# The experts' stage of a mixer-and-experts block: ten precomputed activation blocks spread over 64 groups, and loaded into another tensor

## The chip, the cores and the metric

The kernel runs on one core of a Trainium2 chip. The metric is device time in microseconds, the median of three runs. Besides, one execution was profiled, and the rows below are from it. Engines are named as in the profile: PE (TensorE), DVE (VectorE), ACT (ScalarE), POOL (GpSimd) and SP (SyncE, whose queue issues most plain loads and stores).

## The reference, cut to what matters

One layer: a token mixer, a LayerNorm, and a feed-forward part that retrieves single-neuron experts. Only the last concerns us. With `x` the 1024 tokens of width 1024 behind the first LayerNorm, each token picks 128 of 16384 experts (8 heads, 16 each) with gates, and

```python
def expert_block(args):
    xb, eb, gb = args
    h = jnp.einsum('td,ted->te', xb.astype(f32), u[eb].astype(f32))
    a = jax.nn.gelu(h, approximate=False) * gb
    return jnp.einsum('te,ted->td', a, v[eb].astype(f32))
```

The output is LayerNorm(alpha * x + that), with float32 throughout.

## The kernel before

**Two ways for two halves of the tokens.** The kernel treats 512 tokens sparsely and 512 densely. The four tiles of 128 sparse tokens gather their U and V rows from HBM, one row for each token and picked expert: `gather_u` and `gather_v` on POOL's queue, 128 rows of 4 KB (512 KB) in one indirect DMA. VectorE forms the dot products with the U rows (`dot_rows`, L2147), TensorE sums the V rows of three tiles (`weigh_rows`, L2001, one step for each four gathers), and VectorE those of the last tile (`sum_rows`, L2156). U rows have a ring of 4 buffers and V rows one of 8.

The 512 dense tokens go through all 16384 experts, with gates that are zero where an expert wasn't picked. The experts are cut into 128 blocks of 128, two to a group, so there are 64 groups. In a group `g`, for `j` = 0 and 1:
- SP loads the U block (512 KB) into `e_ur`, ScalarE and VectorE split it into a high part `e_uh` (L2029) and a low part `e_ul` (L2101), one group ahead. TensorE forms the hidden product in 24 matmuls (`hidden`, L1953 to L1955: high x high, high x low, low x high), and ScalarE its Gelu into `e_a` (L2046).
- VectorE multiplies by the gates (`weigh`, L2117), which SP loads as one 512 KB block into `e_g`. ScalarE and VectorE split the product in `e_a` (L2041, L2122).
- SP loads the V block (512 KB) into the single `e_vr`, which is split likewise (L2035, L2105).
- TensorE multiplies the two and VectorE adds eight PSUM banks into `e_y` (`values`, L1986 to L1988, 48 matmuls a group, run one group later; `gather`, L2137).

**What is computed ahead.** 20 of the 128 blocks (`AHEAD`) have had their hidden product and Gelu before this stage, in the retrieval (12) and the gates' stage (8), where they are stored to the scratch tensor `hidden` in HBM. In the kernel before these are blocks 0 to 19, and so groups 0 to 9 (`SHORT` = 10) are short: their `weigh` takes the activations from `e_ur`, where SP loads two blocks of 256 KB (`load_u`, L1859), and TensorE, ScalarE and VectorE skip the product, the Gelu and the splits of U. From group 10 on `load_u` fetches the U blocks (L1864).

**The order of work.** The groups run in the order of their numbers, and each engine has its instructions for a group written out by hand. The rows of the sparse tiles are spread over four phases of the groups, `PHASE = (0, 18, 36, 53, 64)`: in the first three phases each group gets some seven U gathers with their dot products and some seven V gathers, and at a phase's end the sums are turned into the next tile. In the last phase VectorE sums the V rows of the fourth tile, some 12 a group. The SP queue, in order, for each group: the U loads of the next group, the gates, V for `j` = 0, (in the short groups: the next activations), V for `j` = 1. Each waits for the engine that frees the buffer, and holds up what is behind it.

Of the kernel before, what the change touches and what calls it, by code (L numbers as in the profile page):

```python
# [36 lines left out]
TG = 64  # L37
# [17 lines left out]
AHEAD = AHEAD_R + AHEAD_G  # L55
LEVELS = 7

# [1050 lines left out]
def retrieve(nc, sem, io, scr, cst, psum, x1s, x1d, hold, w0, key1, key2, gate):  # L1108
# [3 lines left out]
    with ExitStack() as ctx:  # L1112
# [473 lines left out]
def build_gates(nc, sem, io, scr, cst, psum, x1d, hold, pickT, id_u, hs):  # L1586


    with ExitStack() as ctx:
# [32 lines left out]
        with nc.Block() as block:  # L1622
# [139 lines left out]
def experts(nc, sem, io, scr, cst, psum, x1d, hold, id_u, id_v, gate_s, hs, out):  # L1762
# [3 lines left out]
    with ExitStack() as ctx:  # L1766
# [4 lines left out]
        SHORT = AHEAD // 2  # L1771
# [25 lines left out]
        ln_in = 16 * (NG + 1)  # L1797

        u_in = [sem(f"u_in{j}") for j in range(2)]
        v_in = [sem(f"v_in{j}") for j in range(2)]  # L1800
# [52 lines left out]
        with nc.Block() as block:  # L1853
            @block.sync
            def _(sp):
                def load_u(g, j):
                    if g < SHORT:
                        sp.wait_ge(a_mul[j], g)
                        sp.dma_start(ur[j].rearrange("p k e -> p (k e)")[:, 0:TD],  # L1859
                                     scr["hidden"][2 * g + j]).then_inc(u_in[j], 16)  # L1860
                    else:
                        sp.wait_ge(a_mul[j], SHORT)
                        sp.wait_ge(u_lo[j], g - SHORT)
                        sp.dma_start(ur[j][:], io["uT"][2 * g + j]).then_inc(u_in[j], 16)  # L1864
# [10 lines left out]
                for j in range(2):  # L1875
                    load_u(0, j)
                for g in range(NG):
                    if SHORT < g + 1 < NG:
# [4 lines left out]
                    if g + 1 <= SHORT:  # L1883
                        for j in range(2):
                            load_u(g + 1, j)
                    load_v(g, 1)
                    if g == 0:
                        for t in range(ND):
                            sp.dma_start(y[:, t, :], scr["x1"][TS + t * P:TS + (t + 1) * P, :]).then_inc(x1_in, 16)
                for j, src in enumerate(("ln2_g", "ln2_b")):  # L1890
                    sp.wait_ge(u_lo[j], NG - SHORT)
# [55 lines left out]
            def _(pe):  # L1947
                def hidden(g, j):
                    pe.wait_ge(u_hi[j], g - SHORT + 1)
                    pe.wait_ge(u_lo[j], g - SHORT + 1)  # L1950
                    pe.wait_ge(gelu[j], g - SHORT)
# [61 lines left out]
                for g in range(NG + 1):  # L2013
                    for c in range(V_SLOTS):
                        if c < 2 and SHORT <= g < NG:
                            hidden(g, c)
# [8 lines left out]
            def _(act):  # L2025
                def split_u(g, j):
                    act.wait_ge(u_in[j], 16 * (g + 1))
                    act.wait_ge(h_mm[j], g - SHORT)
# [14 lines left out]
                def activate(g, j):  # L2043
                    act.wait_ge(h_mm[j], g - SHORT + 1)
# [21 lines left out]
                for g in range(NG):  # L2066
# [7 lines left out]
                    for j in range(2):  # L2074
                        if g >= SHORT:
                            activate(g, j)
                        split_a(g, j)
                        if SHORT <= g + 1 < NG:
# [274 lines left out]
```

## Time and profile before

| | us |
|---|---|
| median of 3 runs | 3144.13 |
| lowest and highest | 3140.07, 3150.45 |
| the profiled execution | 3145.47 |
| its span in the profile | 3143.8 |

The span runs from the first to the last instruction that the profile shows. A "busy" time counts instructions of the engine itself, without waits. PE's matmuls overlap, so that a matmul's duration is longer than the distance from its start to the next one's; where the rows below give a length of work on PE or DVE, starts are compared.

### The profile page before, as it was taken

Reading aid. Unit: us, or ns where it says so; the run is one execution under the profiler, and the core shown is the slowest. Engines: PE = TensorE matmul, PEld = TensorE weight load, DVE = VectorE, ACT = ScalarE, POOL = GpSimd, SP = SyncE. Lnnn points to the kernel's source line nnn. Section 1 sums busy time; section 2 is a strip of 40 time slices with the busy share of each in tenths; the row PEclk is TensorE's granted clock in tenths of the full one; section 3 lists DMA queues with packets and bytes.
Section 4 is the critical chain, followed back from the end, with each engine's and each line's share of the span. In section 5 each row is a group of like instructions: output and inputs, shape, how many; then the busy total and the mean of one; then the engine's idle time right before and its main releaser. Section 6 shows DMA issues by size and latency. Waiting matters only on the chain.

```text
span 3143.8 us, 40677 instructions
## 1 busy us (share of the span) xinstructions
PE 2644.5 (84%) x14888; PEld 2060.2 (66%) x14888; DVE 2306.0 (73%) x4891; ACT 1052.3 (33%) x1647; POOL 1616.3 (51%) x1190
## 2 busy tenths in 40 slices
PE   7996688889997466653767999999999999999996
PEld 6886577777775456551445767676767766667775
DVE  4511566655999799984777777777777777879999
ACT  4311333433544477760112222322222222222322
POOL 0001001112887455545666765676665777765774
PEclk9988799999998788886888999999999999999998
DMA  4222412222111599989999999999999999998995
GB/s 137 94 88 79 128 43 85 85 82 74 63 51 33 167 317 310 302 279 365 395 385 386 386 383 347 381 387 388 392 384 341 408 399 407 400 406 297 374 374 202
DMA packets 309791, 833.42 MB, mean 265 GB/s; under 512 B 26112, under 2 KB 114624, under 8 KB 309600
## 3 DMA queue, kind: packets, MB, share of 16 engines
q0 software_dynamic: 150864, 548.60, 45.4%
q1 hardware_dynamic: 158736, 282.31, 25.7%
q8 instruction: 115, 1.88, 0.2%
q14 instruction: 76, 0.62, 0.1%
HBM read 771.93 MB, written 58.88 MB: 264 GB/s over the span
## 4 chain that ended last, share of the span: by engine, by line
DVE 14%; DMA 13%; POOL 12%; PE 9%; issue 7%; ACT 0%; POOLq 0%; DVEq 0%; ACTq 0%
DMA e_u_row<-in_u,ids 13%; POOL hold L1913 8%; POOL e_u_row L1904 4%; DVE e_u_row L2147 4%; DVE e_y L2137 2%; PE psum L1986 2%; DVE e_u_row L2156 1%; PE psum L1987 1%; PE psum L1988 1%; DVE e_vl L2105 1%; DVE e_ul L2101 1%; DVE hold L2156 1%; PE psum L1953 1%; PE psum L1955 1%; PE psum L1954 1%
## 5 line engine op out<-in xcount | busy, mean ns | idle before, releaser
L2147 DVE CUSTOM_DVE_ANT_0 e_u_row<-e_u_row,hold 128x1024 f32<-128x1024 f32 x384 | 467.6, 1222 | 267.9 <-DMA e_u_row<-in_u,ids 267.1
L1904 POOL DMA_INDIRECT e_u_row<-in_u,ids x384 | 489.0, 1273 | 339.9 <-DVE ids L2147 231.6
L1986 PE MATMUL psum<-e_vh,e_ah 128*128 128x512 f32 x1024 | 425.1, 415 | 128.0 <-DVE e_y L2137 95.9
L1913 POOL DMA_INDIRECT hold<-in_v,ids x384 | 442.9, 1153 | 143.9 <-issue 112.8
L1987 PE MATMUL psum<-e_vl,e_ah 128*128 128x512 f32 x1024 | 412.7, 403 | 0.0
L1988 PE MATMUL psum<-e_vh,e_al 128*128 128x512 f32 x1024 | 410.7, 401 | 0.0
L1986 PEld LDWEIGHTS psum<-e_vh,e_ah 128*128 128x128 f32 x1024 | 199.9, 195 | 238.5 <-DVE e_y L2137 131.9
L1953 PE MATMUL psum<-x1d,e_uh 128*128 128x512 f32 x864 | 341.3, 395 | 0.0
L1954 PE MATMUL psum<-x1d,e_uh 128*128 128x512 f32 x864 | 337.2, 390 | 0.0
L1955 PE MATMUL psum<-x1d,e_ul 128*128 128x512 f32 x864 | 336.3, 389 | 0.0
L2137 DVE TENSOR_TENSOR e_y<-e_y,psum 128x512 f32<-128x512 f32 x464 | 299.7, 678 | 20.6 <-PE psum L1988 20.5
L1633 PE MATMUL psum<-g_one,g_two 128*128 128x128 f32 x1024 | 171.0, 345 | 136.9 <-DVE g_one L1676 136.9
L1688 POOL DMA_INDIRECT hold<-in_u,ids x128 | 194.6, 1521 | 173.1 <-DVE ids L1662 125.9
L1633 PEld LDWEIGHTS psum<-g_one,g_two 128*128 128x128 f32 x1024 | 165.9, 258 | 149.8 <-issue 149.8
L2046 ACT ACTIVATE e_a<-psum 128x512 f32<-128x512 f32 x108 | 64.5, 597 | 567.0 <-PE psum L1955 566.9
L2035 ACT ACTIVATE e_vh<-e_vr 128x1024 fp32r<-128x1024 f32 x128 | 135.3, 1057 | 346.3 <-DMA e_vr<-in_v 338.6
L1988 PEld LDWEIGHTS psum<-e_vh,e_al 128*128 128x128 f32 x1024 | 199.8, 195 | 44.9
L1987 PEld LDWEIGHTS psum<-e_vl,e_ah 128*128 128x128 f32 x1024 | 200.3, 196 | 39.4
L1101 POOL TENSOR_TENSOR hold<-hold,m_lng 128x1024 f32<-128x1024 f32 x8 | 18.9, 2362 | 380.7 <-DVE hold L989 380.7
L2001 PE MATMUL psum<-hold,e_column 128*32 128x512 f32 x1536 | 187.8, 607 | 28.3 <-DMA hold<-in_v,ids 21.8
L1953 PEld LDWEIGHTS psum<-x1d,e_uh 128*128 128x128 f32 x864 | 162.3, 188 | 64.4 <-issue 31.0
L2041 ACT ACTIVATE e_ah<-e_a 128x512 fp32r<-128x512 f32 x128 | 80.9, 632 | 347.7 <-DVE e_a L2117 344.2
(399 smaller groups left out, 5648.8 us busy)
## 6 DMA issues: line engine op xcount, KB each, us to landing
e_vr<-in_v SPq DMA_DIRECT2D x128, 512.0 KB, 6.7
e_ur<-in_uT SPq DMA_DIRECT2D x108, 512.0 KB, 6.7
s_G<-g_tile SPq DMA_DIRECT2D x8, 4096.0 KB, 27.0
e_g<-s_G SPq DMA_DIRECT2D x64, 512.0 KB
ids<-in_w_ch SPq DMA_DIRECT2D x17, 512.0 KB, 3.9
s_ch<-p_out POOLq DMA_DIRECT2D x16, 512.0 KB, 4.0
hold<-in_wq SPq DMA_DIRECT2D x16, 512.0 KB, 4.3
hold<-in_v,ids POOLq DMA_INDIRECT x476, 8.5
```

The costliest lines, as they stand in the source:

```text
L1633: last = nc.tensor.matmul(psum[:, n // 4, (n % 4) * NK:(n % 4 + 1) * NK], one2[s][:, n, :], one1[s][:, n, :], start=True, stop=True)
L1688: pool.indirect_dma_start(out=ring[k % U_RING], out_offset=None, in_=io["u"], in_offset=bass.IndirectOffsetOnAxis(ap=id_u[:, 0, k:k + 1], ...
L1904: pool.indirect_dma_start(out=u_ring[n % U_RING][:], out_offset=None, in_=io["u"], in_offset=bass.IndirectOffsetOnAxis(ap=id_u[:, s, k:k + ...
L1913: pool.indirect_dma_start(out=v_ring[m % V_RING], out_offset=None, in_=io["v"], in_offset=bass.IndirectOffsetOnAxis(ap=id_v[:, t:t + 1], a ...
L1953: nc.tensor.matmul(psum[:, j, :], uh[j][:, k, :], x1d[0][:, k, :], start=(k == 0), stop=False)
L1954: nc.tensor.matmul(psum[:, j, :], uh[j][:, k, :], x1d[1][:, k, :], start=False, stop=False)
L1955: last = nc.tensor.matmul(psum[:, j, :], ul[j][:, k, :], x1d[0][:, k, :], start=False, stop=(k == KC - 1))
L1986: nc.tensor.matmul(acc, ah[s][j][:, r], vh[s][j][:, c], start=(first and j == 0), stop=False)
L1987: nc.tensor.matmul(acc, ah[s][j][:, r], vl[s][j][:, c], start=False, stop=False)
L1988: last = nc.tensor.matmul(acc, al[s][j][:, r], vh[s][j][:, c], start=False, stop=(final and j == 1))
L2137: add = nc.vector.tensor_tensor(y[:, t, c], y[:, t, c], psum[:, bank(g, q), :], ALU.add)
L2147: nc.vector.tensor_tensor_reduce(row, row, xs[:, s, :], 1.0, 0.0, ALU.mult, ALU.add, hs[:, s, k:k + 1]).then_inc(dotted, 1)
```

## The change

`READY` names the ten short groups, spread over the stage: 0, 9, 19, 28, 37, 45, 54, 57, 60 and 63. The blocks that the two earlier stages compute ahead are the blocks of these groups (`ready_block`). In the experts' stage `computed(g)` counts the full groups before `g` and takes the place of `g - SHORT` in the semaphores' values. The activations of a short group are loaded by `load_ready` into `e_a` (`av[j]`) itself, when VectorE has finished the last group's subtraction on it (`a_lo`), with semaphores of their own; the product with the gates is then made in place. The two loads stand in the SP queue before and after the second V load. U loads no longer wait for `a_mul`.

```diff
+READY = (0, 9, 19, 28, 37, 45, 54, 57, 60, 63)
+def ready_block(n):
+    return 2 * READY[n // 2] + n % 2
+def computed(g):
+    return g - len([r for r in READY if r < g])
...
-                    sp.dma_start(ur[:], io["uT"][b]).then_inc(u_in, 16)
+                    sp.dma_start(ur[:], io["uT"][ready_block(b)]).then_inc(u_in, 16)
...
-                    sp.dma_start(ur[:], io["uT"][AHEAD_R + b]).then_inc(u_in, 16)
+                    sp.dma_start(ur[:], io["uT"][ready_block(AHEAD_R + b)]).then_inc(u_in, 16)
...
                 def load_u(g, j):
-                    if g < SHORT:
-                        sp.wait_ge(a_mul[j], g)
-                        sp.dma_start(ur[j].rearrange("p k e -> p (k e)")[:, 0:TD],
-                                     scr["hidden"][2 * g + j]).then_inc(u_in[j], 16)
-                    else:
-                        sp.wait_ge(a_mul[j], SHORT)
-                        sp.wait_ge(u_lo[j], g - SHORT)
-                        sp.dma_start(ur[j][:], io["uT"][2 * g + j]).then_inc(u_in[j], 16)
+                    sp.wait_ge(u_lo[j], computed(g))
+                    sp.dma_start(ur[j][:], io["uT"][2 * g + j]).then_inc(u_in[j], 16)
+
+                def load_ready(g, j):
+                    sp.wait_ge(a_lo[j], g)
+                    sp.dma_start(av[j][:], scr["hidden"][2 * READY.index(g) + j]).then_inc(ready_in[j], 16)
...
                 for j in range(2):
-                    load_u(0, j)
+                    load_ready(0, j)
                 for g in range(NG):
-                    if SHORT < g + 1 < NG:
+                    if g + 1 < NG and g + 1 not in READY:
                         for j in range(2):
                             load_u(g + 1, j)
                     load_gates(g)
                     load_v(g, 0)
-                    if g + 1 <= SHORT:
-                        for j in range(2):
-                            load_u(g + 1, j)
+                    if g + 1 in READY:
+                        load_ready(g + 1, 0)
                     load_v(g, 1)
+                    if g + 1 in READY:
+                        load_ready(g + 1, 1)
...
                 def weigh(g, j):
                     dve.wait_ge(g_in, 16 * (g + 1))
-                    if g < SHORT:
-                        dve.wait_ge(u_in[j], 16 * (g + 1))
-                        dve.wait_ge(a_lo[j], g)
-                        src = ur[j].rearrange("p k e -> p (k e)")[:, 0:TD]
+                    if g in READY:
+                        dve.wait_ge(ready_in[j], 16 * (READY.index(g) + 1))
                     else:
-                        dve.wait_ge(gelu[j], g - SHORT + 1)
-                        src = av[j][:]
-                    nc.vector.tensor_tensor(av[j].rearrange("p (b t) -> p b t", t=TG), src.rearrange("p (b t) -> p b t", t=TG),
-                                            gt[:, :, j, :], ALU.mult).then_inc(a_mul[j], 1)
+                        dve.wait_ge(gelu[j], computed(g) + 1)
+                    activation = av[j].rearrange("p (b t) -> p b t", t=TG)
+                    nc.vector.tensor_tensor(activation, activation, gt[:, :, j, :], ALU.mult).then_inc(a_mul[j], 1)
```

Everywhere else on PE, ACT and DVE `SHORT <= g` becomes `g not in READY`, `SHORT <= g + 1 < NG` becomes `g + 1 < NG and g + 1 not in READY`, and `g - SHORT` becomes `computed(g)`.

## Rows read from the trace of the kernel before

**Rows 1.** The page's slices: busy tenths and GB/s in 40 equal parts of the span.
```profile
PE   7996688889997466653767999999999999999996
DMA  4222412222111599989999999999999999998995
GB/s 137 94 88 79 128 43 85 85 82 74 63 51 33 167 317 310 302 279 365 395 385 386 386 383 347 381 387 388 392 384 341 408 399 407 400 406 297 374 374 202
```

**Rows 2.** Windows that start where groups start: stretch, length, busy time and instructions.
```profile
core 0: us, PE busy (x) PEld busy (x) DVE busy (x) ACT busy (x) POOL busy (x), PEclk, DMA share, GB/s
1425.00:1467.30 42.30, 9.21 (x37) 2.79 (x38) 17.25 (x27) 4.14 (x9) 25.15 (x22) 0.54 0.98 375
1467.30:1672.80 205.50, 139.63 (x629) 92.15 (x628) 147.70 (x233) 28.43 (x47) 140.40 (x122) 0.85 1.00 391
1672.80:1707.00 34.20, 22.10 (x86) 16.17 (x85) 21.43 (x34) 6.18 (x9) 21.49 (x18) 0.80 1.02 407
1707.00:1863.00 156.00, 154.29 (x755) 111.88 (x754) 123.91 (x187) 39.43 (x59) 109.64 (x88) 1.00 0.99 387
...
1941.30:2341.70 400.40, 390.87 (x1888) 282.14 (x1881) 311.71 (x471) 103.00 (x153) 274.99 (x225) 0.99 1.00 390
2419.70:2826.40 406.70, 395.03 (x1920) 279.78 (x1913) 317.38 (x481) 103.38 (x154) 291.63 (x238) 1.00 1.02 403
2850.30:3091.70 241.40, 224.85 (x963) 180.09 (x962) 241.10 (x249) 68.30 (x85) 172.59 (x117) 0.99 0.96 357
```

**Rows 3.** The same windows, instructions of L2117 alone, two to a group.
```profile
1467.30:1672.80 205.50, 10.94 (x16) 0.85 1.00 391
1941.30:2341.70 400.40, 20.59 (x30) 0.99 1.00 390
2419.70:2826.40 406.70, 20.61 (x30) 1.00 1.02 403
2850.30:3091.70 241.40, 13.60 (x20) 0.99 0.96 357
```

**Rows 4.** DMA: GB/s in 40 slices of groups 19-33, then 37-51; loads of groups 1-8.
```profile
GB/s 399 405 410 356 411 408 403 347 327 386 409 408 409 408 408 406 248 406 409 408 411 407 408 407 319 339 406 411 409 408 409 408 286 404 406 411 393 409 379 407
...
GB/s 401 370 409 409 408 409 408 406 409 410 404 400 388 411 397 377 410 399 405 412 408 408 409 408 409 407 375 388 400 410 407 410 409 408 411 384 409 411 407 410
...
e_ur<-s_hidden SPq DMA_DIRECT2D x16, 256.0 KB, 6.2
```

**Rows 5.** Timeline of DVE in group 59: start, duration, instruction.
```profile
2999.41 1.21 DVE L2101 TENSOR_TENSOR e_ul<-e_ur,e_uh 128x1024 fp32r<-128x1024 f32 x1
3000.55 1.27 DVE L2156 SCALAR_TENSOR_TENSOR e_u_row<-hold,ids,e_u_row 128x1024 f32<-128x1024 f32 x1
...
3004.07 0.68 DVE L2117 TENSOR_TENSOR e_a<-e_a,e_g 128x512 f32<-128x512 f32 x1
...
3005.87 0.68 DVE L2122 TENSOR_TENSOR e_al<-e_a,e_ah 128x512 fp32r<-128x512 f32 x1
```

**Rows 6.** Timeline of PE: first of 24 hidden matmuls, and the instruction behind them.
```profile
1968.47 0.50 PE L1953 MATMUL psum<-x1d,e_uh 128*128 128x512 f32 x1
...
1974.09 0.39 PE L1986 MATMUL psum<-e_vh,e_ah 128*128 128x512 f32 x1
```

**Rows 7.** Waits of DVE, longest first: groups 19-33, then groups 1-8 (total, times, longest).
```profile
DVE e_u_row L2147 <- DMA e_u_row<-in_u,ids: 74.2, 29, 5.9
...
DVE e_u_row L2147 <- DMA e_u_row<-in_u,ids: 49.1, 18, 8.0
```

**Rows 8.** Timeline of the SP queue in group 9: start, time to issue, load.
```profile
1673.57 12.19 SPq L1864 DMA_DIRECT2D e_ur<-in_uT  x2
1686.10 0.33 SPq L1873 DMA_DIRECT2D e_vr<-in_v  x1
...
1695.01 0.38 SPq L1869 DMA_DIRECT2D e_g<-s_G  x1
```

**Rows 9.** Window of group 21.
```profile
1993.30:2023.30 30.00, 27.97 (x128) 20.42 (x121) 20.17 (x32) 6.70 (x11) 17.00 (x16) 0.94 1.00 380
```

More of the change, by code:

```diff
@@ L1770, in experts @@
         NG = NK // 2
-        SHORT = AHEAD // 2
+        assert 2 * len(READY) == AHEAD
         Q = 2 * ND
@@ L1796, in experts @@
         lng, lnb = (ur[j].rearrange("p k e -> p (k e)") for j in range(2))
-        ln_in = 16 * (NG + 1)
+        ln_in = 16 * (computed(NG) + 1)
         u_in = [sem(f"u_in{j}") for j in range(2)]
+        ready_in = [sem(f"ready_in{j}") for j in range(2)]
         v_in = [sem(f"v_in{j}") for j in range(2)]
@@ L1890, in _ @@
                 for j, src in enumerate(("ln2_g", "ln2_b")):
-                    sp.wait_ge(u_lo[j], NG - SHORT)
+                    sp.wait_ge(u_lo[j], computed(NG))
                     sp.dma_start(ur[j].rearrange("p k e -> p (k e)"), io[src].partition_broadcast(P)).then_inc(u_in[j], 16)
@@ L1948, in hidden @@
                 def hidden(g, j):
-                    pe.wait_ge(u_hi[j], g - SHORT + 1)
-                    pe.wait_ge(u_lo[j], g - SHORT + 1)
-                    pe.wait_ge(gelu[j], g - SHORT)
+                    pe.wait_ge(u_hi[j], computed(g) + 1)
+                    pe.wait_ge(u_lo[j], computed(g) + 1)
+                    pe.wait_ge(gelu[j], computed(g))
                     for k in range(KC):
@@ L2014, in _ @@
                     for c in range(V_SLOTS):
-                        if c < 2 and SHORT <= g < NG:
+                        if c < 2 and g < NG and g not in READY:
                             hidden(g, c)
@@ L2026, in split_u @@
                 def split_u(g, j):
-                    act.wait_ge(u_in[j], 16 * (g + 1))
-                    act.wait_ge(h_mm[j], g - SHORT)
+                    act.wait_ge(u_in[j], 16 * (computed(g) + 1))
+                    act.wait_ge(h_mm[j], computed(g))
                     nc.scalar.activation(uh[j][:], ur[j][:], ACT.Copy).then_inc(u_hi[j], 1)
@@ L2043, in activate @@
                 def activate(g, j):
-                    act.wait_ge(h_mm[j], g - SHORT + 1)
+                    act.wait_ge(h_mm[j], computed(g) + 1)
                     act.wait_ge(a_lo[j], g)
@@ L2074, in _ @@
                     for j in range(2):
-                        if g >= SHORT:
+                        if g not in READY:
                             activate(g, j)
                         split_a(g, j)
-                        if SHORT <= g + 1 < NG:
+                        if g + 1 < NG and g + 1 not in READY:
                             split_u(g + 1, j)
@@ L2099, in split_u @@
                 def split_u(g, j):
-                    dve.wait_ge(u_hi[j], g - SHORT + 1)
+                    dve.wait_ge(u_hi[j], computed(g) + 1)
                     nc.vector.tensor_tensor(ul[j][:], ur[j][:], uh[j][:].bitcast(F32), ALU.subtract).then_inc(u_lo[j], 1)
@@ L2207, in _ @@
                     split_a(g, 0)
-                    if SHORT <= g + 1 < NG:
+                    if g + 1 < NG and g + 1 not in READY:
                         split_u(g + 1, 0)
@@ L2217, in _ @@
                     dot_rows(g, 5)
-                    if SHORT <= g + 1 < NG:
+                    if g + 1 < NG and g + 1 not in READY:
                         split_u(g + 1, 1)
```

## The prediction

> **What bounds the kernel now.** I read the page's slices first, to find the experts' stage and its regimes. It begins at about 1425 us of the span, and from there the DMA engines are shown busy in nine tenths of nearly every slice while TensorE goes from 5 to 7 tenths (the first groups) to 9 [rows 1]. Then I cut the stage into stretches that start where a group's first gating product (L2117) starts; each group has two of them, so the counts say how many groups a stretch holds [rows 2, 3]. The reader is to see three regimes. Groups 1 to 8 have no hidden product to compute: TensorE is busy 139.6 of 205.5 us, VectorE 147.7, and the DMA engines all the time; a group takes 25.7 us. Groups 19 to 33 are all full: TensorE 390.9 of 400.4 us, and the DMA engines all the time again; 26.7 us a group. Groups 37 to 51 are full, with a denser schedule of gathered rows: 27.1 us. In the last regime (groups 53 to 62) VectorE is busy 241.1 of 241.4 us: it sets the pace, at 24.1 us, and TensorE has a little room.
>
> The next view, the DMA answers, tells the two DMA-heavy regimes apart. The fine slices stand at 405 to 412 GB/s wherever nothing interrupts them, and dip now and then; the mean is 390 in groups 19 to 33 and 403 in groups 37 to 51 [rows 4]. So the ceiling here is about 408. Groups 1 to 8, where TensorE is far from its limit, moved 391 [rows 2]: with TensorE out of the way the transfers were not faster. In groups 19 to 33 TensorE and the transfers are both within 5% of their limits. The waits agree: VectorE waits 74.2 us for gathered rows in groups 19 to 33 and 49.1 in groups 1 to 8 [rows 7].
>
> **The change part by part.** Ten groups are short before and ten after, so the work is conserved: per short group TensorE is spared 48 hidden matmuls, ScalarE two splits and two Gelus, VectorE two subtractions, and the SP queue issues two loads of 256 KB instead of two of 512 KB, 0.524 MB less. What moves is the regime in which this is spared: eight from groups 1 to 8, two more in the old run (0 and 9) that stay, and eight new ones: 19 and 28, 37 and 45, and 54, 57, 60, 63.
>
> (a) The last regime. A subtraction takes 1.14 us from its start to the next instruction's start (2999.41 to 3000.55) [rows 5]. Two per group, four groups: 8 x 1.14 = 9.1 us. They fall in iterations 53, 56, 59 and 62, since a group's U block is split one iteration ahead, all of them in the regime where VectorE has no idle time. What comes next: a short group would want 24.1 - 2.3 = 21.8 us; TensorE is spared 11.2 there (below), and the transfers, at 357 GB/s [rows 2], lie under 408 and lose 0.524 MB too. So nothing takes the place: -9.1 us. From below nothing (if something unseen does), and more is excluded, as only these instructions leave the busy engine.
>
> (b) Groups 19 and 28. The 24 hidden matmuls of one j run from 1968.47 to 1974.09, 5.6 us [rows 6], so a group is spared 11.2 us of TensorE. That can't be had in full: VectorE's own work in a short group is 147.7 / 8 = 18.5 us, which leaves 26.7 - 18.5 = 8.2 us at most. From below: if the transfers bind, 0.524 MB at 390 GB/s, 1.3 us. Between the two I take the bytes plus the bandwidth that a group in this regime leaves unused, (408 - 390) / 408 x 26.7 = 1.2 us, as a slack TensorE lets the transfers go through one dip: 2.5 us a group. I stay near the lower end because groups 1 to 8 had all of TensorE's slack and were still only 26.7 - 25.7 = 1.0 us shorter. Two groups: -5.0.
>
> (c) Groups 37 and 45, in the same way: 0.524 MB at 403 GB/s is 1.3 us, unused bandwidth (408 - 403) / 408 x 27.1 = 0.3. 1.6 us each (1.3 to 8.2): -3.2.
>
> (d) Groups 1 to 8 become full. Groups 1 to 15 after the change have the schedule of rows of groups 19 to 33, 18 groups earlier, but for group 9, which is short. So the nearest row is 400.4 us, less one short group at 2.5: 397.9. Before, the same groups took 205.5 + 34.2 + 156.0 = 395.7 [rows 2]: +2.2. The 34.2 in it is group 9: the load of U block 20 waits in the SP queue for the tile that the activations used, the second V load of the group stands behind it until 1686.10, and the next gates go out at 1695.01 [rows 8]. That stall goes. From above, by bytes alone: seven of the eight swaps fall in these groups, 7 x 0.524 = 3.7 MB at 391 GB/s = 9.4 us. I take +3.5, nearer to the lower end, because that row is of the same instructions in the same order; I add a little because group 1 starts with emptier rings than group 19.
>
> (e) The start. The SP queue now has group 1's two U loads ahead of the first gates and V, and no second pair of activations: 0.52 MB more by the end of group 0, at the 375 GB/s of that stretch [rows 2] 1.4 us (0 to 2.8, if all of U's 1.05 MB is waited for).
>
> (f) What costs nothing. In the mixer's later stages only the index of the U block changes. The load of activations now writes the product's tensor, so it waits for the last read of that tensor (the subtraction L2122) instead of the product. In the last regime that is 3005.87 + 0.68 for the second j, and the next product on that tensor comes one group after 3004.07, near 3028 [rows 5]; the load takes 6.2 us [rows 4], so some 15 us cover it. In the SP queue it stands ahead of the second V load, which itself waits for a later VectorE instruction (L2105 of j = 0), and of the next U and gates, which before waited for the second L2101, later still. POOL's order of gathers is untouched, and ScalarE (103.0 us busy in 400.4) hides its part.
>
> The sum: 1.4 + 3.5 - 5.0 - 3.2 - 9.1 = -12.4 us. The profiled execution took 3145.5 us, so 3133.1 by it; it lies 1.3 us above the median of 3144.1, which gives **3132 us**.
>
> **A rule beside (b) and (c).** The dips in the transfer rate end at 408 GB/s and no slice stands above 412 [rows 4]. The Trainium skill (HBM Reference, Access) says that a core streaming alone measures about 425 GB/s, bounded by its DMA engines. By 425 the groups from 37 on would not be at the limit, and TensorE's relief would be worth up to the 8.2 us of (b), the third rival below. The trace doesn't bear it out: 403 GB/s is the mean there, with long runs at 408 to 410.
> The same SP and POOL transfers fill one total in the DMA rows: groups 1 to 8 carry smaller SP loads and are not faster in GB/s [rows 2, 4]. The Trainium skill (DMA: Bandwidth & Descriptors, Issuing engines are not separate DMA queues) says that transfers of all issuing engines run on the same 16 DMA engines and interleave. It speaks against the change, since U blocks only displace gathered rows from one group to another; that is the first rival.
>
> **The rivals.**
> 1. Bytes are conserved and nothing else counts before group 53: (d) 9.4, (e) 1.4, (b) -2.7, (c) -2.6, (a) -9.1: -3.6 us, 3141. For it: 391 and 390 GB/s with and without TensorE's slack. Against it: groups 19 to 33, with 4.2 MB more U data than groups 1 to 15 before, took only 4.7 us longer, not 10.7.
> 2. The forecast, 3132, with a range of its own of 3123 to 3140.
> 3. TensorE is the bound of full groups, and a lone short group between full ones, starting with full rings, gets all that VectorE allows: 4 x 8.2 = 32.8 in (b) and (c). With 4.9 from (d) and (e) and -9.1: -37 us, 3107. For it: TensorE 98% busy; against: groups 1 to 8.
> 4. Slower: TensorE and the transfers are now both tight from group 1 on with cold rings, and the eight groups run like the worst full one, group 21, 30.0 us, in which the rows came late at 380 GB/s [rows 9]. 8 x (30.0 - 25.7) = +34.4, with the rest +1.4 - 17.3: +18.5, 3163. It makes the kernel measurably slower from a mean of 28.9 us in groups 1 to 8.
> 5. The change doesn't do what it says: the activations land late, because their wait sits in the SP queue, and VectorE waits their 6.2 us [rows 4] in each of the ten groups. In the last regime that is 4 x 6.2 in place of a gain of 9.1; with the others at the forecast, +12.4 in all for a wait that counts only there: 3157. The 15 us of cover speak against it.
>
> **How the numbers follow.** What can be told from no change is 0.3%, 9.4 us. Chances: the forecast 0.55, bytes alone 0.25, the third 0.11, the fourth 0.06, the fifth 0.03. Of the forecast's range about 0.08 lies within 9.4 us of the time before. Faster: 0.47 + 0.11 = 0.58; same: 0.25 + 0.08 = 0.33; slower: 0.09. The range takes in the forecast and bytes alone, and half of the third; it leaves out the far side of the third and the last two: 3112 to 3146.
>
> **What would show it.** Groups 53 to 62: VectorE's subtractions L2101 (in the new numbering) fall from 20 to 12 and each iteration ahead of a short group is 2.3 us shorter; if not, look for a wait of VectorE for the new loads. Groups 19 and 28: 24 us or so, with the rate near 408; at 18 to 20 us the third rival is right, at 25.4 the first. Groups 1 to 8: 26.7 us a group, TensorE above 95% and its granted clock at 1.00 instead of 0.85; at 29 the fourth is right. Group 9: no stall of 34. Wrong it would be if rings that a short group empties give the time back in the groups behind it, so that each group's gain is seen but not the stretch's.

## The result, and the profile after

The changed kernel took 3158.99 us (median of seven runs, 3150.88 to 3161.87), the one before 3144.13 (seven runs, 3139.23 to 3150.45): a ratio of 1.0040, with an interval of [1.0029, 1.0051]. It is slower by 0.4%, where 3132 was forecast with a range of 3112 to 3146. The profiled execution took 3161.87 us with a span of 3160.2.

The page's slices of the changed kernel, to be read beside [rows 1]:

```profile
span 3160.2 us, 40569 instructions
PE   7997688889997466653998998998998998998885
DMA  4222412222110599989999999999998999998995
GB/s 137 93 87 72 133 43 84 85 81 72 64 51 32 166 306 308 298 278 361 398 380 388 389 390 344 392 386 380 390 390 329 407 408 400 394 404 306 359 363 201
```

In slices 20 to 22 TensorE now stands at 8 to 9 tenths where it stood at 6 to 7 (not 5 to 7, as the prediction read), so groups 1 to 8 are full, as meant. The GB/s of those slices are what they were.

The next table cuts the span where the first gating product of groups 0, 18, 36, 53 and 63 starts (L2127 in the changed kernel, L2117 before). "Ahead" is all that comes before the experts' stage, "start" the stage up to group 0's first product, "end" is group 63 with the final LayerNorm.

| us | ahead | start | groups 0–17 | 18–35 | 36–52 | 53–62 | end | stage |
|---|---|---|---|---|---|---|---|---|
| before | 1425.4 | 12.5 | 479.5 | 478.4 | 454.6 | 241.3 | 52.0 | 1718.3 |
| before, profiled again (below) | 1431.4 | 11.3 | 477.3 | 475.4 | 452.7 | 243.6 | 52.5 | 1712.8 |
| changed | 1436.2 | 13.3 | 486.9 | 478.1 | 453.8 | 237.0 | 55.0 | 1724.1 |
| changed, profiled again (below) | 1430.7 | 13.6 | 487.1 | 476.7 | 454.1 | 237.9 | 55.0 | 1724.4 |

First the reader is to see that the two profiled spans, 3143.8 and 3160.2, overstate the change. Of their 16.4 us, 10.8 lie ahead of the experts' stage, where only the index of a block differs, and the repeated profiles of the two kernels turn this difference round (1431.4 and 1430.7). Over all profiles of this study "ahead" went from 1421.7 to 1436.2 without regard to the kernel. The stage itself is what the change made longer: from a mean of 1715.6 to 1724.3, +8.7 us, which agrees with the timed +0.4% (12.6 us; the second timing of the same kernel, below, gives 0.28%, 8.8 us).

Windows of the changed kernel: the five stretches of the table and the end; then groups 1 to 8, 9, 18, 19, 28, 37 and 45. The columns are those of [rows 2].

```profile
1436.00:1449.40 13.40, 0.48 (x1) 0.18 (x1) 3.27 (x6) 0.31 (x1) 9.79 (x10) 0.50 0.86 312
1449.40:1936.30 486.90, 445.00 (x2125) 319.33 (x2126) 359.30 (x537) 115.16 (x173) 318.88 (x259) 0.96 0.98 384
1936.30:2414.40 478.10, 447.68 (x2147) 322.05 (x2146) 362.63 (x548) 116.73 (x174) 312.34 (x257) 0.98 0.98 378
2414.40:2868.20 453.80, 425.98 (x2050) 301.40 (x2049) 350.04 (x530) 110.81 (x166) 304.67 (x255) 0.98 1.00 391
2868.20:3105.20 237.00, 196.41 (x796) 156.78 (x796) 232.33 (x241) 56.68 (x69) 171.25 (x117) 0.91 0.96 357
3105.20:3160.20 55.00, 25.22 (x90) 19.14 (x89) 46.79 (x62) 12.34 (x15) 20.58 (x8) 0.75 0.32 124
...
1482.10:1694.50 212.40, 198.14 (x961) 142.09 (x960) 163.15 (x246) 50.06 (x76) 151.40 (x123) 0.98 1.00 392
1694.50:1723.00 28.50, 20.07 (x88) 15.02 (x87) 21.18 (x34) 6.06 (x9) 18.28 (x15) 0.86 1.03 409
...
1936.30:1958.20 21.90, 21.42 (x109) 14.92 (x108) 18.89 (x29) 4.45 (x9) 13.43 (x13) 1.00 0.95 353
1958.20:1985.60 27.40, 19.38 (x90) 13.89 (x92) 21.45 (x35) 6.07 (x9) 19.49 (x17) 0.88 1.02 403
2197.60:2228.70 31.10, 22.27 (x87) 16.19 (x86) 20.36 (x32) 5.99 (x9) 17.98 (x15) 0.78 0.93 358
2436.30:2463.20 26.90, 19.60 (x90) 13.99 (x92) 22.65 (x37) 6.07 (x9) 20.82 (x17) 0.87 1.02 401
2651.10:2680.80 29.70, 20.28 (x88) 14.08 (x90) 21.26 (x34) 6.03 (x9) 19.23 (x16) 0.77 1.03 409
```

The short groups 19, 28, 37 and 45 take 26.9 to 31.1 us each: no less than a full one (26.7 and 27.1 a group [rows 2]), though TensorE is idle for 7 to 9 us in each. The wait view of group 28 shows what closes it:

```profile
DVE e_u_row L2156 <- DMA e_u_row<-in_u,ids: 7.9, 2, 5.9
...
PE psum L1998 <- DVE e_y L2146: 8.8, 1, 8.8
```

VectorE waits for gathered rows first, 5.9 us up to 2204.28, and is late from then on; TensorE waits from 2203.35 to 2212.18 for VectorE to work up to the addition that empties a bank. It is the same in 19, 37 and 45 (7.5, 7.3 and 6.9 us of TensorE's waiting, 5.0, 4.2 and 6.7 of VectorE's). Against the 52.0 us from the last group's first product to the end of the span before, the end is 55.0.

The wait view of VectorE in groups 53 to 62, and the SP queue in the middle of that stretch (start, time to issue, load):

```profile
DVE e_a L2127 <- ACT e_a L2058: 3.0, 3, 1.3
DVE e_a L2127 <- DMA e_g<-s_G: 2.8, 2, 1.5
...
2950.64 0.33 SPq L1875 DMA_DIRECT2D e_a<-s_hidden  x1
2951.01 0.92 SPq L1871 DMA_DIRECT2D e_ur<-in_uT  x2
2952.03 0.38 SPq L1880 DMA_DIRECT2D e_g<-s_G  x1
```

There VectorE is busy 232.3 of 237.0 us, where it had been 241.1 of 241.4 [rows 2]. The subtractions are gone, but 4.7 us of idle time have come, and the queue shows where part of it is from: ahead of short group 57 the gates go out behind both U blocks of group 58, which nothing holds back, as the tile they need is free. 512 KB of gates then land 12.3 us after their issue, behind 1 MB of U, and VectorE has waited 1.5 us for them.

### The profile page after: what moved, and what is told of

Same layout as the page of the kernel before. It is cut to its first block, busy times and chain, and to the rows that moved or that the text cites. A ratio compares the mean times of both kernels' runs of the same rounds, so it can differ in the third digit from the quotient of the medians.

```text
span 3160.2 us, 40569 instructions
## 1 busy us (share of the span) xinstructions
PE 2650.1 (84%) x14888; PEld 2065.6 (65%) x14888; DVE 2308.3 (73%) x4891; ACT 1052.4 (33%) x1647; POOL 1614.3 (51%) x1190
## 4 chain that ended last, share of the span: by engine, by line
DVE 15%; DMA 15%; POOL 10%; PE 8%; issue 6%; ACT 0%; SPq 0%; POOLq 0%; DVEq 0%; ACTq 0%
DMA e_u_row<-in_u,ids 14%; POOL hold L1925 7%; DVE e_u_row L2156 5%; POOL e_u_row L1916 3%; DVE e_y L2146 2%; DVE e_ul L2113 1%; DVE e_vl L2117 1%; PE psum L1998 1%; DVE e_al L2131 1%; DVE e_u_row L2165 1%; DVE hold L2165 1%; PE psum L1999 1%; PE psum L1965 1%; PE psum L2000 1%; PE psum L1966 1%
```

## The experiments

All ratios are to the kernel before, run in alternation on the same chip. Where a kernel has the same code in a stretch as one of the two, its profile is used as one more sample of that stretch.

### Where the loss comes from: the parts one by one

The load path alone, with the ten short groups left at the front:

```diff
-READY = (0, 9, 19, 28, 37, 45, 54, 57, 60, 63)
+READY = tuple(range(10))
```

> The changed kernel with its short groups put back to 0 to 9, so that only the new way of loading the activations (into the product's tensor, waiting for the subtraction, around the second V load) is left of the change. Theory A (the place of the short groups sets the time: eight blocks of U added where gathered rows already fill the transfers, and saved where little can be had): no slower than before, 3138 to 3145 us, group 9 without its 34 us. Theory B (the new load path costs, by queueing in front of V and gates): the slowdown stays, 3150 us or more.

Measured: 1.0009 [0.9995, 1.0024]; groups 0 to 17 took 478.2 us, between the 479.5 and 477.3 of the kernel before. Group 9 fell from 34.2 to 29.1 us, and yet nothing was gained: group 0 became 3 us longer (29.6 to 32.7), and groups 10 to 17 together 1.5 to 2.5. So the new load path as a whole costs nothing, but it isn't free in its parts: in group 0 VectorE waits 3.7 us for the gates of group 1, which now go out behind the second load of activations (at 1463.95, 19 us after group 0's first product; before, 8 us after it). What the stall in group 9 gives is about what group 0 and groups 10 to 17 take.

Four short groups moved to the last stretch, and four moved to the two middle ones, six left at the front:

```diff
+READY = (0, 1, 2, 3, 4, 5, 54, 57, 60, 63)
...
+READY = (0, 1, 2, 3, 4, 5, 19, 28, 37, 45)
```

> Short groups 0 to 5, 54, 57, 60 and 63: half of the eight moves, all into the last regime. Theory A: four more full groups at the start, 4 x 0.524 MB at 391 GB/s, +5.4 us; the last regime -4.4 us as the changed kernel's profile shows it (9.1 less the new waits for gates and Gelu); no later start, since group 1 is short: +1 us, 3145. Theory B: six of ten groups are still loaded singly or in the SP queue's new order; half the slowdown or more, 3150 or more.

> Short groups 0 to 5, 19, 28, 37 and 45. Theory A: +5.4 us at the start and -1 us in the two middle phases, as the changed kernel's profile shows them: +4 us, 3148. If a lone short group among full ones were worth the 2.5 and 1.6 us forecast: -3 us, 3141.

Measured: 1.0018 [1.0006, 1.0030] and 1.0022 [1.0009, 1.0035]. In both, groups 0 to 17 took 486.2 and 486.4 us: four swaps there cost already what eight do. The four in the middle gave nothing: 477.7 and 455.4 us in the two middle stretches. The four at the end gave 238.4 in place of 241.3, and lost 3.2 us again in the end (55.2).

The changed kernel and the one before, once more each (no edit):

> The changed kernel again, beside the others on one chip. Theory A: its experts' stage is longer than that of the kernel before by what the profiles showed (first phase +7, last regime -4, end +3: +6 us), and the stages ahead of it, which differ only in the index of a block, wander from run to run without a sign: 6 to 8 us above the kernel before in the median. Rival: these stages are really slower (+10.8 us in the first profile): 12 us or more, and gates' stage and projection long again.

> The kernel before, for a second profile. If the stages ahead of the experts' wander by chance: they end within 1425 to 1436 us, and not again at the low end; the experts' stage within 2 us of 1718.4. If the index of the blocks computed ahead matters: 1425 again.

Measured: 1.0028 [1.0018, 1.0038] and 0.9995 [0.9979, 1.0010]; their stretches stand in the table above.

### Groups 0 to 17: bytes, TensorE or VectorE

Three kernels that leave out one thing each in the groups that became full, then combinations. The U loads of groups 2 to 8 are halved; TensorE computes 12 of the 48 hidden matmuls in groups 1 to 8; VectorE subtracts an eighth of each U block of groups 2 to 8:

```diff
+                    part = slice(0, KC // 2 if 2 <= g <= 8 else KC)
+                    sp.dma_start(ur[j][:, part, :], io["uT"][2 * g + j][:, part, :]).then_inc(u_in[j], 16)
...
+                    for k in (0, KC - 1) if 1 <= g <= 8 else range(KC):
...
+                    k = slice(0, 1 if 2 <= g <= 8 else KC)
+                    nc.vector.tensor_tensor(ul[j][:, k, :], ur[j][:, k, :], uh[j][:, k, :].bitcast(F32),
+                                            ALU.subtract).then_inc(u_lo[j], 1)
```

> The changed kernel with only half of each U block loaded in groups 2 to 8 (256 of 512 KB; the other half of the tile keeps what stood there, so the products of these groups are not the reference's). TensorE, ScalarE and VectorE do the same instructions; the transfers carry as much as in short groups. Theory A1 (bytes): the first phase, 486.9 us as changed and 478.2 with short groups 0 to 9, loses 7 x 0.524 MB at 391 GB/s, 9 us, and comes to 478. Rival A2 (TensorE is the bound of the full groups): it stays near 487. In between if both bind.

> The changed kernel with 12 instead of 48 hidden matmuls in groups 1 to 8 (six of the eight slices of the sum are left out, so the products of these groups are not the reference's). The loads and splits stay. Theory A1 (bytes): the first phase stays at 486 to 487 us. Rival A2 (TensorE): 8 x 36 x 0.23 us = 66 us of TensorE's work go, and the phase falls to the 478 of short groups or below.

> Half U loads in groups 2 to 8 and 12 instead of 48 hidden matmuls in groups 1 to 8 together (left out: half of these U blocks and six of eight slices of the products of these groups). Alone the first gave 482.7 us in the first phase and the second 490.2, where the changed kernel takes 487. Theory A3 (transfers and TensorE bind at nearly the same level, so that either alone gives half or nothing): together 478 as with short groups 0 to 9. Rival A4 (what is left, VectorE's two subtractions a group and the order of the loads in the queue, holds the phase): 482 or more.

> The changed kernel with VectorE's subtraction of U in groups 2 to 8 cut to an eighth of the tile (the rest of the low part keeps old values, so the products of these groups are not the reference's). Loads and matmuls stay. Theory A5 (the first phase is VectorE's own order of work: its waits for rows stay near 100 us whatever bytes or matmuls are taken away, since the ring of four rows lets them come no earlier, so that work added to VectorE is added to the phase): 7 x 2 x 1.0 us of subtractions go, and the phase falls from 487 to 478 or so. Rival A1 (bytes): stays at 486 to 487, with VectorE's waits for rows longer by as much.

> Half U loads, 12 of 48 hidden matmuls and an eighth of the subtractions in groups 2 to 8 at once (matmuls also in group 1; left out is what the three single runs left out). If these three are all that a full group has more than a short one: the first phase at 478, as with short groups 0 to 9. Above 482, the number and order of the loads and the wait for the Gelu are what is left.

Measured: half of U 1.0015 [1.0005, 1.0024], few matmuls 1.0026 [1.0012, 1.0039], both 1.0009 [0.9993, 1.0024], few subtractions 1.0032 [1.0016, 1.0048], all three 1.0009 [0.9992, 1.0025]. The windows of groups 0 to 17 tell more, the columns as above: of half of U, of few matmuls, of both, of few subtractions, of all three.

```profile
1445.20:1927.90 482.70, 445.23 (x2125) 318.42 (x2126) 359.16 (x537) 115.43 (x173) 314.13 (x258) 0.96 0.98 379
```
```profile
1442.20:1932.30 490.10, 399.39 (x1837) 277.18 (x1838) 358.97 (x537) 114.69 (x173) 312.81 (x259) 0.90 0.98 381
```
```profile
1446.80:1930.50 483.70, 399.55 (x1837) 276.34 (x1838) 359.13 (x537) 114.81 (x173) 317.50 (x259) 0.91 0.98 379
```
```profile
1440.10:1926.90 486.80, 445.61 (x2125) 319.66 (x2126) 345.93 (x537) 114.99 (x173) 306.61 (x259) 0.96 0.98 384
```
```profile
1435.60:1917.20 481.60, 399.33 (x1837) 274.34 (x1838) 345.82 (x537) 114.41 (x173) 310.99 (x259) 0.91 0.98 379
```

TensorE is 45 us less busy in the second row, although its granted clock fell with the work (0.96 to 0.90), and the stretch is no shorter; VectorE 13 us less busy in the fourth, and no shorter either: neither sets the pace. Only the rows with half of U are shorter, 482.7, 483.7 and 481.6, against a mean of 486.3 (484.8 to 487.1) in the three profiles with the changed kernel's code there. What VectorE does with the time that it is spared shows in its longest wait, for gathered rows, over groups 0 to 17: first the changed kernel profiled again, then few subtractions.

```profile
DVE e_u_row L2156 <- DMA e_u_row<-in_u,ids: 97.5, 35, 13.7
```
```profile
DVE e_u_row L2158 <- DMA e_u_row<-in_u,ids: 113.0, 37, 12.1
```

13 us of work less, some 15 us more of waiting for rows.

So about half of the loss, 486.3 - 482.7 = 3.6 us of 7.9 (from 478.4, the mean of the three profiles with ten short groups in front; 482.7 is also the mean of the three with half of U), goes with U's bytes. The other half is still open: half of U moves 482.7 us x 379 GB/s = 182.9 MB, less than the 184.1 MB of the kernel before (479.5 us at 384 GB/s, the window of the whole stretch), and takes longer, at a lower rate.

### Groups 53 to 62, and the end

The gates of a short group are loaded ahead of the next group's U blocks:

```diff
                 for g in range(NG):
+                    if g in READY:
+                        load_gates(g)
                     if g + 1 < NG and g + 1 not in READY:
                         for j in range(2):
                             load_u(g + 1, j)
-                    load_gates(g)
+                    if g not in READY:
+                        load_gates(g)
```

> The changed kernel, with the gates of a short group issued ahead of the next group's two U loads instead of behind them. Theory A: of VectorE's waits in the last regime those for the gates (2.8 us in two groups) go, and the rest of the kernel is as changed: 3 us less than the changed kernel, about 3153 to 3156. If the gates' lateness is also what stalls the groups in the other phases: 6 us less or more.

Measured: 1.0027 [1.0014, 1.0040]. Groups 53 to 62 took 235.6 us (without this edit 238.0, mean of nine profiles), and the wait for gates is gone from VectorE's list. 3.9 us of waits for the Gelu stay. The timing doesn't show the gain: the changed kernel itself had 1.0028 and 1.0040, and in this kernel's profile groups 18 to 35 took 483.5 us, longer than in any other here (477.3 with the same order of loads in the last experiment of the next part).

POOL's additions in the final LayerNorm are held back until VectorE has finished the multiplications of all sparse tiles:

```diff
-                    pool.wait_ge(nrm_g, t + 1)
+                    pool.wait_ge(nrm_g, max(t + 1, NS - 1))
```

> The changed kernel with POOL's first LayerNorm addition held back until VectorE has made its three multiplications in a row. Theory A7 (of the 2.8 us that the last stretch is longer since group 63 is short, 2.2 is VectorE's third multiplication, 3.42 instead of 1.22 us while a POOL addition runs beside it): that instruction takes 1.22 us again and the last stretch 52.5 to 53.0 us instead of 55.0. Rival (the length is of the data or of the load of the weights): 3.4 us stays.

Measured, in one execution: 3150.16 us beside 3145.39 for the kernel before, and an end of 52.5 us instead of 55.0. Two rows of the timeline for each of the changed kernel, the kernel before and this one: VectorE's multiplications by the LayerNorm's weight, three in a row, and POOL's additions.

```profile
3123.89 5.69 DVE L2197 TENSOR_TENSOR hold<-hold,e_ur 128x1024 f32<-128x1024 f32 x3
...
3125.26 8.87 POOL L1956 TENSOR_TENSOR hold<-hold,e_ur 128x1024 f32<-128x1024 f32 x3 [22.68 <-DVE hold L2197]
```
```profile
3109.62 3.49 DVE L2188 TENSOR_TENSOR hold<-hold,e_ur 128x1024 f32<-128x1024 f32 x3
...
3110.99 9.08 POOL L1944 TENSOR_TENSOR hold<-hold,e_ur 128x1024 f32<-128x1024 f32 x3 [21.90 <-DVE hold L2188]
```
```profile
3114.03 3.49 DVE L2197 TENSOR_TENSOR hold<-hold,e_ur 128x1024 f32<-128x1024 f32 x3
...
3117.67 7.09 POOL L1956 TENSOR_TENSOR hold<-hold,e_ur 128x1024 f32<-128x1024 f32 x3 [24.37 <-DVE hold L2197]
```

Without POOL beside it VectorE needs 3.49 us for three, and POOL without VectorE 7.09. In the kernel before POOL alone pays for the meeting (9.08); in the changed kernel VectorE pays 2.2 us (5.69) and POOL 1.8 (8.87). VectorE is on the path that ends the kernel. All ten profiles with a short group 63 and POOL not held back have an end of 54.3 to 55.2 us, the nine others without it 52.0 to 52.5.

### Where a short group is worth something

The nine short groups after group 0 are all put in the last stretch, with the gates first:

```diff
+READY = (0, 54, 55, 56, 57, 58, 59, 60, 61, 62)
```

> Short groups 0 and 54 to 62, gates issued ahead of U behind a short group. VectorE's regime gets nine short groups, and none of them has U loads in front of its gates: 9 x 2.3 = 20.5 us less there. Group 63 stays full: the last stretch keeps its 52.0 us instead of 55.0. The first phase is as in the changed kernel, +8 us, with group 9 full another 1 us, the two middle phases as before. Theory A: -11 us, 3134. If other waits (for rows, for V) take the place of VectorE's subtractions in a row of short groups: no faster than before.

> The version with short groups 0 and 54 to 62, again, for a narrower interval. By its profile against the two of the kernel before, its experts' stage is 1710.2 us against 1718.4 and 1712.9, 5.5 us shorter: a ratio of 0.9982, and at most 0.9995. Were the first interval (0.9977 to 1.0) luck: 1.0 or above.

Measured: 0.9988 [0.9977, 1.0000], and timed again 0.9986 [0.9974, 0.9998], 3141.36 us beside 3145.39. This beats both kernels, by little: the second interval ends just below 1. The windows of groups 53 to 62 and of the end, second profile:

```profile
2859.90:3084.50 224.60, 149.23 (x530) 115.25 (x529) 220.89 (x231) 40.79 (x48) 166.77 (x117) 0.83 0.97 367
3084.50:3136.60 52.10, 27.21 (x117) 21.27 (x115) 44.57 (x62) 12.94 (x16) 20.80 (x8) 0.82 0.33 122
```

The stretch is 17.2 us shorter than the 241.9 that the kernel before's code takes (mean of the seven profiles without a short group there; in the first profile of this version 15.2 us). Nine groups spare 18 subtractions, 20.5 us by the forecast's price; VectorE is still nearly always busy. Groups 0 to 17, without their nine short groups, took 489.3 and 485.3 us and take most of it back.

In groups 18 to 35, where the changed kernel has two short groups, eight are placed in a row (21 to 28), and then as every other group; the third kernel is the second with the first hidden product of the next group moved, in TensorE's order, ahead of the last half of the value matmuls that run in a short group (those of the group before it):

```diff
+READY = (0, 21, 22, 23, 24, 25, 26, 27, 28, 45)
...
+READY = (0, 20, 22, 24, 26, 28, 30, 32, 34, 45)
...
                     for c in range(V_SLOTS):
-                        if c < 2 and g < NG and g not in READY:
+                        if c < 2 and g < NG and g not in READY and not (c == 0 and g - 1 in READY):
                             hidden(g, c)
+                        if c == 3 and g in READY and g + 1 < NG and g + 1 not in READY:
+                            hidden(g + 1, 0)
```

> Short groups 0, 21 to 28 and 45: eight in a row in the second phase. Theory A (short groups are worth bytes and TensorE together, and only in a row, since what one spares comes in three different groups: the U load two groups ahead, the split one group ahead, the product in the group itself): the second phase falls by what eight were worth in the first, 9 us, to 469; the first as in the previous experiment with one short group, 489. Rival (nothing to gain in that phase anywhere): 477.

> Short groups 0, 20, 22, 24, 26, 28, 30, 32, 34 and 45: eight in the second phase, none next to another. Theory A (a lone short group is worth little): the second phase falls by less than half of what eight in a row give, to 474 or stays. Rival (by bytes, wherever they lie): 8 x 0.524 MB at 390 GB/s, 10.7 us, 467.

> Short groups 0, 20, 22, 24, 26, 28, 30, 32, 34 and 45 as before, with the first hidden product of the group behind a short one moved up in TensorE's order, ahead of the second half of the short group's values. Theory A6 (a lone short group's time is lost because TensorE waits for VectorE's bank additions in its place, 52.7 us in eight waits in the second phase, and the next hidden product and Gelu stand behind that): VectorE's waits for the Gelu fall from 34.5 to 20 us or less and the second phase from 477.6 to about 468, what eight in a row gave. Rival A1 (the transfers bind there anyway): the waits move to the rows and the phase stays at 475 or more.

Measured: in a row 1.0020 [1.0004, 1.0036], every other 1.0047 [1.0033, 1.0062], every other with the early product 1.0025 [1.0010, 1.0040]. Groups 18 to 35 took 468.4, 477.6 and 470.5 us; without any short group there they took 476.5 (mean of six profiles, 474.1 to 478.4). The waits of TensorE and VectorE over groups 18 to 35, of every other first, then with the early product:

```profile
PE psum L1998 <- DVE e_y L2146: 52.7, 8, 11.6
...
PE psum L1998 <- DVE e_vl L2117: 10.2, 6, 4.3
...
DVE e_u_row L2156 <- DMA e_u_row<-in_u,ids: 73.5, 32, 6.6
DVE e_a L2127 <- ACT e_a L2058: 34.5, 17, 6.4
```
```profile
PE psum L1998 <- DVE e_vl L2119: 32.5, 6, 7.1
PE psum L1998 <- DVE e_y L2148: 22.8, 7, 5.5
...
DVE e_u_row L2158 <- DMA e_u_row<-in_u,ids: 100.3, 33, 9.1
DVE e_a L2129 <- ACT e_a L2060: 4.7, 3, 2.0
```

In the first, TensorE has the time that it was spared and spends it waiting: in each of the eight short groups its last value matmuls need a bank that VectorE's additions haven't emptied, and the next group's hidden product, which needs none of that, stands behind them. So that product is late, its Gelu too, and VectorE waits 34.5 us for Gelus (20.7 in the first experiment's same stretch, with no short group). Eight in a row, TensorE waits for these additions just as long (52.2 us), but VectorE only 17.7 us for Gelus: it is the late product that costs, not TensorE's waiting. With the product moved ahead the wait for Gelus is 4.7 us, though TensorE still waits 55.3 us for VectorE (62.9 before), now mostly for the low part of V. In the place of the Gelus comes the wait for rows, and 7 of the 30 us are left as gain. That is one profile each, in a stretch where profiles of the same code lie up to 8 us apart; the timed ratios, 1.0047 and 1.0025, differ by as much (some 7 us), with intervals that overlap a little.

The same early product, with the gates first, in the changed kernel:

> The changed kernel with that order of TensorE's work and with the gates ahead of U behind a short group. Theory A6: groups 19 and 28, 37 and 45 now give 1 to 2 us each, the last regime loses its waits for gates and Gelu (5.8 us as changed): 6 to 9 us less than the changed kernel, near the kernel before, 3147 to 3150. Rival A1: only the last regime's part, 3 to 4 us.

Measured: 1.0039 [1.0023, 1.0054]. Groups 53 to 62 took 235.0 us, the best of the ten-group spread, but the middle stretches 477.3 and 454.5, no less than before. Where the gain went is seen in TensorE's wait for VectorE's additions in group 29, behind short group 28, and in group 46, behind 45:

```profile
PE psum L2001 <- DVE e_y L2151: 4.1, 1, 4.1
...
PE psum L2001 <- DVE e_y L2151: 7.5, 1, 7.5
```

In the short groups themselves that wait is gone (8.8 and 6.9 us as changed, now none and 0.2), and they are shorter, 28.4 and 26.6 us instead of 31.1 and 29.7. But the groups behind them, in which TensorE had waited none and 1.1 us, are longer: 29.1 and 31.5 instead of 26.7 and 27.7. The same wait has moved behind 19 and 37 as well (4.6 us in group 20, 6.3 in group 38). So for lone groups far apart the early product only moves the wait one group on.

## Why the prediction was wrong, step by step

The sum was -12.4 us; the two profiles of each kernel show +8.7 for the stage. The measured terms below are differences of means over all profiles whose work in that stretch is that of the changed kernel or of the kernel before; the stretches are those that the terms were worked out for.

| step | forecast | measured | from profiles (changed, before) |
|---|---|---|---|
| (e) start and group 0 | +1.4 | +4.2 | 3, 2 |
| (d) groups 1–15 | +3.5 | +6.9 | 3, 2 |
| groups 16 and 17 | none | -2.1 | 3, 2 |
| (b) groups 18–35 | -5.0 | -0.3 | 9, 6 |
| (c) groups 36–52 | -3.2 | +0.2 | 9, 6 |
| (a) groups 53–62 | -9.1 | -3.9 | 9, 7 |
| the end | none | +2.7 | 10, 9 |
| sum | -12.4 | +7.7 | |

**(b) and (c) failed outright**, and they carry 8.1 of the 20.1 us between the sums. "A slack TensorE lets the transfers go through one dip" was the step; a lone short group gives nothing, not even its bytes. The price of 2.5 us was taken for a group as if it were spared everything at one time. In the rows after, what is spared comes apart: U's load and its split drop out one group earlier and the product in the group itself. Group 18, with nothing to split for 19, takes 21.9 us where it took 24.0, and group 19 then 27.4 where it took 26.0. In the lone short group VectorE waits for gathered rows, and TensorE's 7 to 9 us then end in one wait for VectorE. The prediction's own last sentence named this end, emptied rings that "give the time back in the groups behind it": as changed, the time is given back in the short group itself, and with the early product in the group behind. The forecast's measure was groups 1 to 8, eight in a row, and in a row short groups pay in groups 18 to 35 too: 8.1 us for eight, about 1 us each, by one profile. Every other one pays nothing there, because the next hidden product stands in TensorE's order behind a wait for VectorE, and its Gelu is late: the early product, which changes only that order, took VectorE's waits for Gelus from 34.5 to 4.7 us. What is left of it as gain, about 7 us, is known only roughly.

**(d) had the right row and the wrong credit.** Groups 1 to 8 run at 26.6 us a group and TensorE's clock is granted at 0.98 of its higher level (2.4 GHz), nearly as said. By the row of groups 19 to 33 they would take 213.5 us, and groups 10 to 15 160.2; they took 212.8 and 159.7 (means of three profiles). But group 9, priced by that row less the 2.5 us of a lone short group at 24.2 us, took 29.0. That is the same failed price as in (b). So the eight groups that became full cost 7.5 us, close to the bound by bytes (9.4) that was named and set aside, and the end of group 9's stall gave back 4.7 of the 10 us that were counted on. As to why the full groups cost that: for groups 0 to 17, 7.9 us in all, halving U's loads gives back 3.6 us; sparing TensorE or VectorE, nothing. What the other half is, was not found: neither the bytes (fewer than before in that experiment), nor TensorE, nor VectorE, nor all three together, which stayed at 481.6 against 478.4. And it isn't in proportion: four swaps cost as much as eight.

**(a) had the right mechanism**: 8 subtractions fell out (12 in place of 20, 14.60 us), iterations 53 and 62 are 2.3 us shorter (26.1 to 23.8 and 23.7 to 21.4), and VectorE's busy time fell by 8.8 us. Of the 9.1 only 3.9 arrived; iterations 56 and 59 are but 0.8 and 0.9 us shorter. The step that failed is in (f), where the new order in the SP queue was said to be without a price: the next U and gates were said to have waited longer before. The U loads behind a short group now wait for nothing, go out as a burst, and the gates stand behind them. Gates first gives 2.4 us (238.0 to 235.6), and iterations 56 and 59 are then 2.3 and 1.7 us shorter than before. The other 2.8 us are about what VectorE's wait for Gelus grew by (1.3 us before, 3.9 with the gates first); the early product left 3.6 of it, so what makes the Gelu late there stays open.

**The end** was not in the sum at all. A short group 63 lets VectorE and POOL meet in another order in the final LayerNorm, and the one that is held up now is VectorE: +2.2 us in its multiplications, and some 0.5 in a wait for TensorE. Holding POOL back removes most of it (52.5 us, in one execution).

**(e)** had the wrong reason. Up to the end of group 0 it forecast +1.4 us (0 to 2.8) for U's bytes; 4.2 came (45.7 instead of 41.5), and 3.5 of it (45.0) come in the load path alone too, where group 1 is short and no U stands ahead of the gates. There it is the gates of group 1, issued late, that VectorE waits for; in the changed kernel they go out later still, behind the U loads of group 2, but VectorE's waits for gates are only 1.7 us there, and what makes up the rest stays open. It is again (f)'s queue order that was not free. As (f) said, the loads of the activations land in time: no wait of VectorE for them appears in groups 53 to 62, and the load path alone measures 1.0009, so the fifth rival is out. (Its sum kept the gain that its words replace: -12.4 + 24.8 is +12.4; with 24.8 in place of the 9.1 it would have been +21.5.) Of the others, bytes alone (3141) had (b), (c) and (a) at -14.4 us where -4.0 came; the third, all of TensorE's relief, falls with the lone groups, in which TensorE idles for 7 to 9 us and nothing is gained, and with the 45 us of the few matmuls that moved nothing. (The 425 GB/s beside it stand in the Trainium skill under HBM Reference, Specifications (TRN2), not under Access.) The fourth had the sign and its mechanism was not there: groups 1 to 8 took 26.6 us a group, not 30.

## What to carry to other kernels

What a group of work is spared counts only if all of it falls where the pace is set: here a subtraction on the always busy VectorE was worth most of its duration, and 11 us of TensorE and 0.5 MB in a lone group nothing, as TensorE then waited for another engine, in that group or, with its work in another order, in the one behind. When a load loses its wait, look at what stands behind it in the same queue: a burst with nothing to hold it back delays the small urgent load behind it. And compare a stretch by several profiles of the same code before pricing 2 us in it; groups 18 to 35 with the changed kernel's work ranged from 470.5 to 478.4 in nine profiles.

## What was not expected of the hardware

A VectorE multiplication over 128x1024 takes 1.22 us alone and up to 3.42 with POOL's addition of the same size beside it, and that addition takes 2.36 alone and up to 4.36 (the first of the three in the kernel before). The view by line shows VectorE's in the changed kernel (shortest, median and longest of four, in ns):

```profile
L2197 DVE TENSOR_TENSOR hold<-hold,e_ur x4: 1219/1222/3416, 3123.9 to 3137.4; 128x1024 f32<-128x1024 f32 x4
```

The Trainium skill (SBUF — State Buffer, Who interferes with whom) says that VectorE and GpSimd share one pair of SBUF ports under an exclusive lock, and that only this pair contends. The trace agrees in kind: each loss is about the rest of the other's instruction (2.2 us of VectorE's against 2.36 of POOL's addition). Which of the two is held up stays open: POOL's first addition starts 1.37 us after VectorE's first multiplication in both kernels (3125.26 - 3123.89, 3110.99 - 3109.62), and by the times VectorE's third multiplication gets in ahead of it before (1.21 us) and waits for it after (3.42 us).
